# Rounded products of two units ahead of the low ones, weight pieces placed earlier at layer boundaries, and the inverse's turn moved in a decoder step on one core

## The reference, cut to what matters

```python
def _layer(x, pos, st, lp):
    h = _rmsnorm(x, lp['norm_mix_pre'])
    y, new_st = _token_mixers(h, pos, st, lp)
    x = x + _rmsnorm(y, lp['norm_mix_post'])
    h = _rmsnorm(x, lp['norm_mlp_pre'])
    u = jnp.square(jax.nn.relu(jnp.einsum('btd,df->btf', h, lp['w_up'])))
    x = x + _rmsnorm(jnp.einsum('btf,fd->btd', u, lp['w_down']), lp['norm_mlp_post'])
    return x, new_st
...
        A = jnp.where(strict, dec_in, 0.0) * bc[..., :, None] * jnp.einsum('bhid,bhjd->bhij', kc, kc)
        rhs = jnp.concatenate([(bc * gam)[..., None] * kc, bc[..., None] * vc], axis=-1)
        sol = lax.linalg.triangular_solve(eye + A, rhs, left_side=True, lower=True, unit_diagonal=True)
```

## Time and profile before

| | us |
|---|---|
| median of 3 executions (3137.81 to 3142.33) | 3140.09 |
| profiled execution, its own time | 3140.11 |
| its span in the trace | 3138.6 |
| PE busy | 3054.0 (97%) |
| DVE busy | 1919.4 (61%) |
| ACT busy | 1542.6 (49%) |
| POOL busy | 85.6 (3%) |

### The profile page before, as it was taken

The page is one execution under the profiler, slowest core; times in us unless marked ns, Lnnn a source line. Parts: engine busy times, 40 slices in busy tenths (PEclk is TensorE's granted clock), DMA queues, the critical chain, the costliest instruction groups (busy, mean ns, idle before and its releaser), DMA issues.

```text
span 3138.6 us, 66992 instructions
## 1 busy us (share of the span) xinstructions
PE 3054.0 (97%) x23012; PEld 2985.0 (95%) x23012; DVE 1919.4 (61%) x3994; ACT 1542.6 (49%) x3580; POOL 85.6 (3%) x163
## 2 busy tenths in 40 slices
PE   8999999999999999999999999999999999999998
PEld 7999999998999999999989999999989999999997
DVE  6677776656545545455576777766565454554555
ACT  6476665545333334334455676655454333343343
POOL 1100000000000000000001000000000000000000
PEclk9999999999999999999999999999999999999999
DMA  6554445553544444444445444455535445444444
GB/s 210 178 153 138 140 140 157 168 180 127 170 165 161 165 162 167 161 162 166 155 142 177 146 145 143 138 163 159 171 129 167 160 163 167 165 162 166 163 164 155
DMA packets 267255, 499.96 MB, mean 159 GB/s; under 512 B 34528, under 2 KB 39936, under 8 KB 267072
## 3 DMA queue, kind: packets, MB, share of 16 engines
q1 hardware_dynamic: 244224, 443.64, 43.9%
q0 software_dynamic: 14784, 51.05, 4.7%
q10 hardware_dynamic: 8064, 2.80, 0.3%
HBM read 475.38 MB, written 22.01 MB: 158 GB/s over the span
## 4 chain that ended last, share of the span: by engine, by line
PE 80%; DVE 11%; ACT 5%; issue 3%; DMA 1%; ACTq 0%; DVEq 0%; POOL 0%; SPq 0%; POOLq 0%
PE PU L523 72%; PE PABCD L523 3%; DVE WL L1300 2%; PE PE_ L523 2%; PE PF L523 2%; ACT AE L899 1%; ACT Y L899 1%; DVE AE L1687 1%; ACT WH L899 1%; DMA RAW<-in_w 1%; DVE Y L1484 1%; DVE Y L1320 1%; DVE X L1327 0%; DVE HL L1305 0%; DVE AM L1592 0%
## 5 line engine op out<-in xcount | busy, mean ns | idle before, releaser
L523 PE MATMUL PU<-HH,WH 128*128 128x288 f32 x4000 | 1236.4, 309 | 29.5 <-DVE HL L1305 21.1
L899 ACT ACTIVATE WH<-RAW 128x512 fp32r<-128x512 f32 x1669 | 965.4, 621 | 583.4 <-PE PU L523 436.6
L1300 DVE TENSOR_TENSOR WL<-RAW,WH 128x512 fp32r<-128x512 f32 x1668 | 1077.1, 687 | 271.1 <-ACT WH L899 258.0
L523 PE MATMUL PU<-HL,WH 128*128 128x288 f32 x4000 | 1183.2, 296 | 0.0
L523 PE MATMUL PU<-HH,WL 128*128 128x288 f32 x4000 | 1180.2, 295 | 0.0
L523 PEld LDWEIGHTS PU<-HH,WH 128*128 128x128 f32 x4000 | 754.4, 189 | 61.1 <-issue 41.6
L523 PE MATMUL PU<-UH,WH 128*128 128x288 f32 x2560 | 759.1, 297 | 2.8 <-DVE UL L1475 1.9
L523 PEld LDWEIGHTS PU<-HL,WH 128*128 128x128 f32 x4000 | 755.9, 189 | 4.1
L523 PEld LDWEIGHTS PU<-HH,WL 128*128 128x128 f32 x4000 | 755.9, 189 | 0.0
L523 PE MATMUL PU<-UL,WH 128*128 128x288 f32 x2560 | 755.2, 295 | 0.0
L523 PE MATMUL PU<-UH,WL 128*128 128x288 f32 x2560 | 752.6, 294 | 0.0
(11 more groups left out here) (281 smaller groups left out, 2214.7 us busy)
## 6 DMA issues: line engine op xcount, KB each, us to landing
RAW<-in_w SPq DMA_DIRECT2D x1669, 256.0 KB, 3.8
SIN<-in_sin POOLq DMA_DIRECT2D x32, 512.0 KB, 4.9
out_sout<-Y POOLq DMA_DIRECT2D x32, 512.0 KB, 5.4
BC<-gate_rows POOLq DMA_DIRECT2D x32, 304.0 KB, 4.4
AUX<-in_aux POOLq DMA_DIRECT2D x32, 152.0 KB, 3.2
X<-in_x SPq DMA_DIRECT2D x4, 576.0 KB, 8.6
out_y<-X SPq DMA_DIRECT2D x8, 288.0 KB, 2.1
out_sout<-SOUT ACTq DMA_DIRECT2D x32, 64.0 KB, 2.4
```

The costliest lines, as they stand in the source:

```text
L523: return nc.tensor.matmul(out, lhsT, rhs, start=start, stop=stop, skip_group_check=True)
L899: return nc.scalar.activation(out, in_, f, **kw)
L1300: tt(WL[s % 2][:, k], RAW[c][:], WH[s % 2][:, k].bitcast(F32), ALU.subtract).then_inc(sem("lo_ready"), 1)
```

## The change

1. A new function `pair_part` replaces `SIDE_BY_SIDE` in "up_first" and in "first" of layer 1: an even slot does WH·HH and WL·HH of two chunks for both units (8 products), the odd slot behind it WH·HL of the same chunks for both units (4 products). It waits for `hh_ready` in the one and `hl_ready` in the other. Both units now end in slot 15.
2. At the boundaries `hi_part` and `lo_part` of piece 4 stand ahead of the norm's scale, and pieces 5, 6, 7 behind groups 1, 3, 5 on both engines; VectorE's piece at the end goes.
3. ScalarE's multiplication of the last chunk of Y by the norm's weight (`weigh`) stands behind Ln and Exp of `norm_scale`; VectorE waits for it in group 7 alone.
4. The transpose of XM stands in slot 3, right behind XM, and writes Q2 in place of XT.
5. The first load of NG0 is started by ScalarE in place of GpSimd, with a semaphore of its own.

```diff
@@ tensor
+            def pair_part(Q, t, kind, l):
+                kk, low = divmod(t, 2)
+                e = 2 * l + (1 if kind == "up_first" else 0)
+                if t == 0:
+                    pe.wait_ge(sem("psum_read"), 4 * Q + 2)
+                if not low and kk % 2 == 0:
+                    pe.wait_ge(sem("lo_ready"), 16 * Q + 4 + kk // 2 + 1)
+                for s in range(2):
+                    psum = PU[s][:, 0:T]
+                    for k in (2 * kk, 2 * kk + 1):
+                        if s == 0:
+                            pe.wait_ge(sem("hl_ready" if low else "hh_ready"), e * NC_ + k + 1)
+                        if low:
+                            last = mm(psum, WH[s][:, k], HL[:, k], False, k == NC_ - 1)
+                        else:
+                            mm(psum, WH[s][:, k], HH[:, k], k == 0, False)
+                            mm(psum, WL[s][:, k], HH[:, k], False, False)
+                    if t == 15:
+                        last.then_inc(sem("unit_done"), 1)
...
-                        mm(PD[:, a:b], xt, XT[:, a:b])
+                        mm(PD[:, a:b], xt, Q2[:, a:b])
@@ scalar
+            act.dma_start(NG0[:], d["ng0"][0]).then_inc(sem("gain_at_start_in"), 16)
...
-                    if (e or l) and g in (0, 1, 3, 5):
-                        hi_part(Q, (g + 1) // 2 + 4)
+                    if (e or l) and g in (1, 3, 5):
+                        hi_part(Q, g // 2 + 5)
...
             def after_out(l):
+                Q = l * QUADS + HEADS + NC_ // 4
+                hi_part(Q, 4)
                 norm_scale(2 * l + 1, RS, "rs_ready")
-                prenorm(l, 2, NG[:, 1], l * QUADS + HEADS + NC_ // 4)
+                weigh(l, 0, NC_ - 1)
+                prenorm(l, 2, NG[:, 1], Q)
 
             def after_mlp(l):
+                if l < DEPTH - 1:
+                    hi_part((l + 1) * QUADS, 4)
                 norm_scale(2 * l + 2, RS, "rs_ready")
+                weigh(l, 2, NC_ - 1)
@@ vector
                     dve.wait_ge(sem("gdn_root"), 2 * nk + 1)
+                    nc.vector.transpose(Q2, XM).then_inc(sem("gdn_root_turned"), 1)
                     tt(NX, EYES[:], XM, ALU.subtract).then_inc(sem("gdn_root"), 1)
...
-                if t == ROOT_SLOT:
-
-                    dve.wait_ge(sem("kv_turned"), n + 1)
-                    dve.wait_ge(sem("gdn_root"), 2 * nk + 1)
-                    nc.vector.transpose(XT, XM).then_inc(sem("gdn_root_turned"), 1)
...
             def update_and_split(l, which, lo_l, lo_which, lo_gain, Q):
 
+                lo_part(Q, 4)
                 for g in range(8):
                     scale_y(l, which, g)
                     if g != 1:
...
                     if g in (1, 3, 5):
-                        lo_part(Q, g // 2 + 4)
+                        lo_part(Q, g // 2 + 5)
                 prenorm_lo(lo_l, lo_which, lo_gain, range(14, 16))
-                lo_part(Q, 7)
```

More of the change, by code:

```diff
@@ L80 @@
 LAST_SLOTS = {0: 0, 1: 1, 2: 3, 3: 6, 10: 8, 4: 9, 5: 9, 8: 11}
-SIDE_BY_SIDE = [(t % 2, t // 2) for t in range(16)] + [divmod(t, 8) for t in range(16, SLOTS)]
 JOINED = [(0, kk) for kk in range(7)] + [(1, kk) for kk in range(7)] + [(0, 7), (1, 7)] + [divmod(t, 8) for t in range(16, SLOTS)]
@@ L477, in store_rows @@
                 pool.dma_start(NG0[:], d["ng0"][l + 1]).then_inc(sem("first_gain_in"), 16)
-            pool.dma_start(NG0[:], d["ng0"][0]).then_inc(sem("first_gain_in"), 16)
             load_gate_weights(0)
@@ L514, in _ @@
                     load_gate_weights(l + 1)
-            pool.wait_ge(sem("first_gain_in"), 16 * (DEPTH + 1))
+            pool.wait_ge(sem("first_gain_in"), 16 * DEPTH)
             pool.wait_ge(sem("state_out"), 16 * DEPTH * HEADS)
@@ L526, in turn @@
                 return nc.tensor.transpose(out, in_, IDENT)
+            def pair_part(Q, t, kind, l):
[17 more added lines that the diff above has]
+                        last.then_inc(sem("unit_done"), 1)
             def unit_part(Q, t, kind, l, x, joined):
-                s, kk = JOINED[t] if joined else SIDE_BY_SIDE[t] if two_at_once(kind, l) else divmod(t, 8)
+                if two_at_once(kind, l) and t < 16:
+                    pair_part(Q, t, kind, l)
+                    return
+                s, kk = JOINED[t] if joined else divmod(t, 8)
                 hi, lo = (UH, UL) if kind in ("out", "down", "down0", "down_last") else (HH, HL)
@@ L781, in gdn_head @@
                     for (a, b, m), xt in zip(TILES, (XM[:, 0:HD], XM[:, HD:SEQ], XM_S)):
-                        i = mm(PD[:, a:b], xt, XT[:, a:b])
+                        i = mm(PD[:, a:b], xt, Q2[:, a:b])
                     i.then_inc(sem("gdn_root_square"), 1)
@@ L916, in prenorm @@
             def prenorm(l, e, gain, Q):
-                if e == 0:
-                    act.wait_ge(sem("first_gain_in"), 16 * (l + 1))
-                else:
+                if e:
                     act.wait_ge(sem("gains_in"), 16 * (l + 1))
+                elif l:
+                    act.wait_ge(sem("first_gain_in"), 16 * l)
                 which = e // 2
@@ L927, in prenorm @@
                         act.wait_ge(sem(f"x_in{g // 2}"), 16)
+                        act.wait_ge(sem("gain_at_start_in"), 16)
                     for c in (2 * g, 2 * g + 1):
@@ L972, in output_squares, with weigh @@
                     act.wait_ge(sem("gains_in"), 16 * (l + 1))
-                gain = NG[:, 0 if kind == "out" else 2, c:c + 1]
-                fn(Y[:, c], Y[:, c], scale=gain).then_inc(sem("output_squares"), 1)
+                if c < NC_ - 1:
+                    weigh(l, 0 if kind == "out" else 2, c)
+            def weigh(l, which, c):
+                fn(Y[:, c], Y[:, c], scale=NG[:, which, c:c + 1]).then_inc(sem("output_squares"), 1)
             def norm_scale(count, dst, name):
@@ L1312, in scale_y @@
                     dve.wait_ge(sem("rs_ready"), e + 1)
-                    dve.wait_ge(sem("output_squares"), 2 * NC_ * (e + 1))
+                    dve.wait_ge(sem("output_squares"), 2 * NC_ * (e + 1) - 1)
                     for c in range(2):
@@ L1319, in scale_y @@
                 k = slice(2 * g, 2 * g + 2)
+                if g == 7:
+                    dve.wait_ge(sem("output_squares"), 2 * NC_ * (e + 1))
                 tt(Y[:, k], Y[:, k], RS[:].unsqueeze(1).to_broadcast([128, 2, T]), ALU.mult).then_inc(sem("y_scaled"), 1)
```

4 lines of the change are left out of this document (1 added, 3 removed).

## The result

The changed kernel takes 3151.56 us (median of 7 executions, 3149.95 to 3155.14), the kernel before 3140.97 beside it (7 executions, 3137.81 to 3142.33): ratio 1.0035, 95% interval 1.0026 to 1.0045, so slower by 0.35%. The profiled execution took 3151.81 us, its span is 3150.3.

The account below looks back on a forecast made before the run. TensorE (busy 97% of the span) bounds the kernel, VectorE the boundaries' end. Heads -8.8, boundaries +17.2, clock +2.8, start -0.2 sum to +11.0 us on 3140.11: forecast 3151 us, range 3140 to 3157.

Parts of the forecast that it names:

- heads: 16 gated-delta heads: the transpose wait partly becomes a wait for the identity addition; 0.55 us less each, 8.8 in all.
- boundary up_first, layer 0: Boundary to up_first in layer 0: VectorE's waits add 7.14 us, tail shrinks from 5.44 to 3.0; 4.7 us later.
- boundary to layer 1: "first" of layer 1: gates' matmul starts later, 7.14 us of waits less 0.6 for the piece gone; 6.5 us.
- boundary up_first, layer 1: Boundary to up_first in layer 1: VectorE's waits add 7.14 us, tail shrinks from 4.10 to 3.0; 6.0 us later.
- clock: TensorE's granted clock falls after waits up to 2.6 us in both up_first; 0 to 5.6 us, 2.8 taken.
- start: Kernel start: ScalarE's first piece no longer waits for NG0; 0 to 0.9 us less, 0.2 taken.
- sum: All terms together: -8.8 + 17.2 + 2.8 - 0.2 = +11.0 us, giving 3151 us.
- The piece that waits for its own group: Boundaries: VectorE's `lo_part` waits for ScalarE's `hi_part` in the same group; 2.38 us idle, nine times.
- The rule that the addition can follow only the weight piece: Heads: the identity addition on VectorE starts no earlier than the weight piece's end, 275.52; so 0.5 to 0.55 of 1.19 us won.
- The tail: Both up_first: the third unit starts 3.0 us behind the end of HL, rounded products being done ahead.
- The tail before: Kernel before, end of HL to third unit's start: 5.44 us in layer 0, 4.10 in layer 1, subtracted as won.
- The chain of transfers: Boundary to layer 1: VectorE's last update instruction, GpSimd's transfers, ScalarE, then the gates' matmul; starts 6.5 us later.

Follow-up runs that it names:

- the pieces alone: The kernel before with only the new order of the weight pieces at the boundaries (part 2); 3158.90 us, ratio 1.0057.
- the pair order alone: The kernel before with only TensorE's new product order, `pair_part` (part 1), pieces in the old order; 3148.57 us, ratio 1.0024.
- turn: The kernel before with only the transpose of XM moved right behind XM, into Q2 (part 4); 3131.24 us, ratio 0.9969.
- heads: The kernel before with two edits in the gated-delta heads: transpose right behind XM, identity addition ahead of slot 5's weight piece; 3122.32 us, ratio 0.9935.
- start: The kernel before with only NG0 loaded from ScalarE's queue (part 5); 3144.12 us in one execution.
- start with loads held: The kernel before with part 5, and GpSimd's two gate-weight loads held until X's first quarter landed; 3144.44 us in one execution.
- The run with SIN held: The changed kernel with GpSimd's load of the states at layer 1's start held until the fourth unit's first low part; 3152.22 us in one execution.
- the kernel with the addition first: The changed kernel with ScalarE's pieces 5 to 7 a group ahead and the heads' identity addition ahead of slot 5's weight piece; 3120.73 us, ratio 0.9932.

## Why the prediction came out right, and where its steps were off

| term | predicted | measured |
|---|---|---|
| heads | -8.8 | -9.5 |
| boundary up_first, layer 0 | +4.7 | +4.9 |
| boundary to layer 1 | +6.5 | +7.9 |
| boundary up_first, layer 1 | +6.0 | +6.2 |
| clock | +2.8 | 0 beyond what is in the rows above |
| start | -0.2 | +1.2 |
| a late RAW load in layer 0 | none | +0.8 |
| sum | +11.0 | +11.5 by these rows, 11.7 by the spans |

*The piece that waits for its own group* was the right mechanism. The wait was 2.22 us (2.30 in the distance from addition to piece, predicted 2.38), it shrank by what was taken from between (0.67 us), and vanished with the order, nine times.

*The heads.* The rule that the addition can follow only the weight piece held: taken away, the other half of the 19.2 us came. A head gave 0.59 us, not 0.55; the sum, 9.5, lies outside the 7 to 8.8 on which the range was built.

*The tail.* I put it at 3.0 us and it was 3.2. The reason that I gave, rounded products done ahead, isn't shown: the pieces alone give 3.3 (4.7 where the clock was low), the pair order alone 6.2.

*The tail before* is where up_first's two terms owe something to the execution that I read. I subtracted 5.44 us in layer 0 and 4.10 in layer 1, as if the layers differed. They don't: in the five kernels that leave this boundary alone (before, turn, heads, start, start with loads held) five of ten tails are 4.08 to 4.10, with a granted clock of 1.00, and five are 5.44 to 5.47, with 0.50 at their beginning; each kernel but the turn alone and the start with held loads has one of each. All twelve tails of the kernels that have the new piece places and the pair order are 3.21 to 3.24. Against the turn alone, layer 0's boundary costs 4.9 + 1.3 = 6.2 us, as much as layer 1's. That +4.9 and +6.2 match +4.7 and +6.0 so closely is because forecast and measurement use the same execution of the kernel before.

*The boundary to layer 1* was mis-sized by 1.4 us. The chain of transfers came nearly as predicted, 5.8 us later for 6.5 (ScalarE's GP at 1598.31, TensorE's matmul of the gates at 1603.16, 7.7 us later where the boundary had started 1.9 us later). I had left out that RAW for the fourth unit, asked for later, then lies beside GpSimd's loads. The run with SIN held shows the part of that load and those behind it: 2.3 us of ScalarE's wait.

*The clock* was the term that failed. I took 2.8 us, half of 5.6, because I expected waits of up to 2.6 us in one go. The 2.8 us for each up_first were my estimate, and no run shows them. What the runs show in their place: the tail of the old order took 5.44 to 5.47 us with 0.50 granted at its beginning and 4.08 to 4.10 at 1.00, and both tails of the changed kernel had 1.00. Its waits came divided: in each round TensorE waited at most 1.33 us for HL and 0.67 and 0.21 us for HH. In layer 0 the granted clock was low only at the beginning of the boundary (0.56 and 0.87 in 727 to 733, above), and 1.00 from 733 us on, third unit included; in layer 1 it was 0.58 and 0.85 in 2297 to 2303, and 1.00 from there on. So the change cost no clock at the end of these boundaries, and in layer 0 it saved some: the kernel before was granted 0.50 behind its wait of 1.96 us there.

*The start* had the wrong sign. I had written that GpSimd's loads go earlier too, and priced it at less than nothing: the first piece won 1.0 us, and the second, which sets the pace, lost 1.2.

The errors cancelled. The forecast was 2.8 us too slow by the clock and 0.7 by the heads, 3.5 in all; it was 1.4 too fast at the boundary to layer 1, 1.4 at the start, 0.8 by the late load and 0.4 in the two up_first, 4.0 in all. The main mechanism was right, but a forecast within 1 us owes that to luck.

## What to carry to other kernels

When two engines share a step (one rounds, the other takes the rest), read for each group which engine comes to it first: an engine that must wait for its neighbour on the same group stops everything queued behind it (2.22 us nine times here), and with the neighbour a group ahead these waits were gone. Before a tail or a boundary is priced to 1 us, read it in more than one execution: here the same code gave 4.1 or 5.5 us. When a wait is removed, look for what stands ahead of the next instruction of that chain: here one line moved past a weight piece was worth as much as the edit that was made. An early transfer can be paid for by those beside it: moving a small one out of a queue also moved the large ones behind it forward, by 0.7 and 0.55 us here, and a load beside them landed 1.2 us later.

## What the runs showed of the hardware

- The same wait in the same code was followed by either clock. In the five kernels that leave up_first's boundary alone, TensorE waits 1.96 to 1.99 us for the last weight piece in nine of ten cases (1.69 in the tenth). The granted clock behind it fell to 0.50 in five of the nine and stayed at 1.00 in the others, and the tail was 5.4 to 5.5 us or 4.1. With the pieces alone, all four waits of 3.00 or 3.01 us for HL (two in each up_first) had 0.50 behind them at some point; those of 1.53 and 1.54 us had 1.00. The changed kernel's waits of 1.14 to 1.33 us had 1.00 from 733 us on. But waits as short are no safeguard: with the states held, layer 1's boundary had a wait of 1.33 us at 2311.50, and the clock fell to 0.50 from 2314 to 2317, which cost nothing there, since TensorE waited for HL again behind it. Pieces alone, layer 0:

```profile
750.62 0.61 PE L523 MATMUL PU<-HH,WH 128*128 128x288 f32 x1 [3.00 <-DVE HL L1308]
```

```profile
736.00:739.00 3.00, 3.00 (x17) 0.66 0.26 84
739.00:742.00 3.00, 2.77 (x16) 0.77 0.00 0
...
751.00:754.00 3.00, 3.00 (x16) 0.50 0.21 70
```

- At the start of layer 1's first "out" quad ten of thirteen profiles show 1.00. The other three are the changed kernel with the states held (0.66 and 0.91, above), the start alone (0.77 and 0.80 in two stretches of 4 us), and the profiled execution of the kernel with the addition first:

```profile
2178.00:2182.00 4.00, 2.50 (x14) 0.74 0.48 137
2182.00:2186.00 4.00, 4.00 (x19) 0.50 0.46 166
2186.00:2190.00 4.00, 4.00 (x29) 0.90 0.52 165
```

  Part of it may be a wait ahead: TensorE waits there for VectorE, 0.90, 0.67 and 1.50 us in these three and 0.40 to 0.92 in the ten. As 0.92 went with 1.00 and 0.67 with 0.77, the wait alone doesn't decide it. In the last of the three 4 x (0.26 + 0.50 + 0.10) = 3.4 us at a clock of 1.00 are missing, partly in idle time, beside its +3.2 us at the last boundary. So one execution places a boundary to about 3 us only.
- At the start, two loads of 512 KB from GpSimd's queue, started 0.7 and 0.55 us earlier, went with a landing of a 256 KB load of SyncE's queue 1.2 us later (12.03 against 10.82; 11.92 to 12.13 in the six kernels with the new start, 10.82 to 11.45 in the six with the old one). At the boundary to layer 1 a load of 256 KB landed 4.80 us after its issue in place of 7.08 when a load of 512 KB and those behind it were held.
